# Attention probabilities turned by VectorE blocks and transfers instead of TensorE transposes, with the heads spread over the next group

## The reference

```python
def masked_softmax(s, mask):
    s = jnp.where(mask, s.astype(jnp.float32), NEG_INF)
    m = jnp.max(s, axis=-1, keepdims=True)
    p = jnp.exp(s - m) * mask
    return p / jnp.maximum(jnp.sum(p, axis=-1, keepdims=True), TINY)

p_c = masked_softmax(s_c, cmp_end[None, :] <= t[:, None])
o_c = jnp.einsum('bgrsc,bgcd->bgrsd', p_c.astype(vc.dtype), vc)
...
o = g[..., 0:1] * to_heads(o_c) + g[..., 1:2] * to_heads(o_s) + g[..., 2:3] * to_heads(o_w)
```

## Time and profile before

| | |
|---|---|
| median of 3 executions | 2071.82 us (2071.75 to 2071.89) |
| profiled execution | 2071.25 us |
| its span, first to last instruction | 2069.6 us |
| mean granted TensorE clock | 0.998 |
| busy: PE / PEld | 2050.0 / 1703.5 us |
| busy: DVE / ACT / POOL | 1352.3 / 972.7 / 168.6 us |
| read from memory | 379.91 MB, 185 GB/s over the span |

### The profile page before, as it was taken

How to read it: one execution, slowest core, us unless ns; L and a number is a source line. 1 busy time by engine, 2 the same in 40 slices (tenths; PEclk the granted TensorE clock), 3 DMA queues, 4 the chain that set the end, 5 groups by cost and what they waited for, 6 DMA issues and landing times.

```text
span 2069.6 us, 27656 instructions
## 1 busy us (share of the span) xinstructions
PE 2050.0 (99%) x9586; PEld 1703.5 (82%) x9586; DVE 1352.3 (65%) x1783; ACT 972.7 (47%) x1261; POOL 168.6 (8%) x263
## 2 busy tenths in 40 slices
PE   8999999999999999999999999999999999999997
PEld 7788888888888888888888888888888888888886
DVE  6755667666664578886678876766546646655664
ACT  5443545454543455554455544544434434444443
POOL 3000000000000011111011110110000000100000
PEclk9999999999999999999999999999999999999999
DMA  8656464545466656666656567676666666666663
GB/s 268 215 160 199 133 182 141 165 141 167 143 205 198 176 175 186 181 182 201 186 171 183 183 211 255 217 217 215 215 195 213 213 194 194 223 202 180 227 213 134
DMA packets 197145, 396.19 MB, mean 191 GB/s; under 512 B 13408, under 2 KB 13504, under 8 KB 195632
## 3 DMA queue, kind: packets, MB, share of 16 engines
q1 hardware_dynamic: 188656, 364.42, 57.1%
q0 software_dynamic: 8208, 29.75, 4.7%
q10 hardware_dynamic: 176, 0.53, 0.1%
HBM read 379.91 MB, written 2.16 MB: 185 GB/s over the span
## 4 chain that ended last, share of the span: by engine, by line
PE 94%; DVE 2%; issue 2%; ACT 1%; DVEq 0%; DMA 0%; POOLq 0%; POOL 0%; ACTq 0%
PE acc L294 29%; PE acc L296 29%; PE acc L295 29%; PE x L918 1%; PE tr L329 1%; DVE lo L261 1%; PE x L854 1%; PE tr L876 1%; DMA raw<-w_proj_ssm 0%; PE x L861 0%; PE tr L878 0%; PE tr L869 0%; PE tr L881 0%; PE x L930 0%; PE x L329 0%
## 5 line engine op out<-in xcount | busy, mean ns | idle before, releaser
L261 DVE TENSOR_TENSOR lo<-raw,hi 128x1024 fp32r<-128x1024 f32 x688 | 839.3, 1233 | 490.0 <-ACT hi L255 481.1
L255 ACT ACTIVATE hi<-raw 128x1024 fp32r<-128x1024 f32 x688 | 718.6, 1058 | 655.4 <-PE acc L296 610.3
L294 PE MATMUL acc<-hi,LAh 128*128 128x512 f32 x1848 | 734.8, 398 | 1.2 <-DVE lo L261 1.2
L296 PE MATMUL acc<-hi,LAl 128*128 128x512 f32 x1848 | 721.4, 390 | 0.0
L295 PE MATMUL acc<-lo,LAh 128*128 128x512 f32 x1848 | 720.6, 390 | 0.0
L294 PEld LDWEIGHTS acc<-hi,LAh 128*128 128x128 f32 x1848 | 347.3, 188 | 74.0 <-issue 3.6
L296 PEld LDWEIGHTS acc<-hi,LAl 128*128 128x128 f32 x1848 | 347.0, 188 | 72.9
L295 PEld LDWEIGHTS acc<-lo,LAh 128*128 128x128 f32 x1848 | 347.4, 188 | 71.7 <-issue 1.7
L294 PE MATMUL acc<-hi,LBh 128*128 128x512 f32 x896 | 350.1, 391 | 0.7 <-DVE lo L261 0.7
L296 PE MATMUL acc<-hi,LBl 128*128 128x512 f32 x896 | 349.0, 389 | 0.0
L295 PE MATMUL acc<-lo,LBh 128*128 128x512 f32 x896 | 348.9, 389 | 0.0
(11 more groups left out here) (304 smaller groups left out, 1210.6 us busy)
## 6 DMA issues: line engine op xcount, KB each, us to landing
raw<-w_in SPq DMA_DIRECT2D x304, 512.0 KB, 3.8
raw<-w_up SPq DMA_DIRECT2D x128, 512.0 KB, 4.0
raw<-w_down SPq DMA_DIRECT2D x128, 512.0 KB, 4.7
raw<-w_proj_ssm SPq DMA_DIRECT2D x64, 512.0 KB, 4.6
raw<-w_proj_nsa SPq DMA_DIRECT2D x32, 512.0 KB, 4.4
raw<-w_out SPq DMA_DIRECT2D x32, 512.0 KB, 5.1
W<-acs_rows POOLq DMA_DIRECT2D x8, 1024.0 KB, 5.0
W<-TB POOLq DMA_DIRECT2D x48, 128.0 KB, 4.2
```

What stands on the lines that cost most here:

```text
L255: act.activation(hi[:, sl, :, :], raw[:, sl, :, :], ACT.Copy).then_inc(s_hi, 1)
L261: dve.tensor_tensor(lo[:, sl, :, :], raw[:, sl, :, :], hi[:, sl, :, :].bitcast(F32), ALU.subtract).then_inc(s_lo, 1)
L294: pe.matmul(o, xh, wh, start=(k == 0), stop=False)
L296: x = pe.matmul(o, xl, wh, start=False, stop=(k == KT - 1))
```

## The change

PE's transposes of the probabilities go. `PB` now holds, for each half of the tokens, four blocks of 128 keys (the compressed ones, `PC`, are the last block). DVE's `scale_probs` becomes `factors` (only the small operations), ACT scales (`scale_probs`, four instructions), and DVE turns the 32x32 blocks (`turn_probs`, two instructions). POOL issues four transfers of 128 KB for each head (`spread_probs`) that put the blocks on their partitions in `PTS`, which `values` reads through an access pattern of runs of 32 numbers. There is one `PTS` for three groups (in BCT) and one for the last (Y), and the block transposes go to BCT, then TH, then V3.

The steps of a head are spread: after the scores in slot s come the maxima and exponentials in s + 1, the factors in s + 3, the scaling in s + 4, the block transposes in s + 5 and the values in s + 9. Steps beyond slot 31 fall into the next group (`late`). The scores stand in slots 12, 19, 25 and 30, in the last group in 12, 17, 22 and 27. The convolution's turn moves from slot 18 to 17. ACT, DVE and POOL have the stage written out instead of looping.

```diff
-SL_S, SL_PT, SL_PV = (12, 16, 20, 25), (16, 20, 25, 29), (17, 22, 27, 31)
-SL_Q, SL_BC = 10, 18
+SL_S = ((12, 19, 25, 30),) * 3 + ((12, 17, 22, 27),)
+A_MAX, A_SUM, A_MUL, A_TURN, A_PV = 1, 3, 4, 5, 9
+SL_Q, SL_BC = 10, 17
...
+        PC = PB[:, :].rearrange("p (b m k) -> p b m k", b=2, m=4)[:, :, 3, :]
+        PBT = [BCT[:, 8:12, :].rearrange("p k s -> p (k s)")] * 9 + [TH.rearrange("p a s -> p (a s)")] * 3 + [V3[:, 0:2, :].rearrange("p n c -> p (n c)")] * 4
+        PTS = [BCT[:, 12:16, :].rearrange("p k s -> p (k s)")] * 3 + [flat_y]
...
+            def spread_probs(n):
+
+                pool.wait_ge(s_pb, n + 1)
+                if n:
+                    pool.wait_ge(s_tr, 2 * (E_AT + EPV + 6 * ((n - 1) // 4) + (n - 1) % 4) + 2)
+                for a in range(4):
+                    pool.dma_start(PTS[n // 4][:, S * a:S * (a + 1)],
+                                   PBT[n][32 * a:32 * (a + 1), :].rearrange("i (b n) -> i b n", b=4)).then_inc(s_ps, 16)
...
-            def turn_probs(i, r, e):
-                pe_event(pe, e, [(s_p, 4 * i + r + 1)])
+            def values(i, r, e):
+
+                pe_event(pe, e)
+                pe.wait_ge(s_stage, 5 * i + 5)
+                pe.wait_ge(s_ps, 64 * (4 * i + r + 1))
+                pt = PTS[i].rearrange("p (a b m j) -> p b m a j", a=4, b=2, m=4)
                 for b in range(2):
-                    pe.transpose(TR[b][:, 0:P], PB[:, 512 + P * b:512 + P * (b + 1)], identf[:, :])
-                    for k in range(2):
-                        pe.transpose(TR[b][:, P * (k + 1):P * (k + 2)], PB[:, S * b + P * k:S * b + P * (k + 1)], identf[:, :])
-                    pe.transpose(TR[b][:, 384:512], PC[:, b, :], identf[:, :]).then_inc(s_tr, 1)
...
-                    pe.matmul(TR[0][:, 0:S], VSs[:, 0, b, :], PTS[:, b, 0:S], start=(b == 0), stop=False,
+                    pe.matmul(TR[0][:, 0:S], VSs[:, 0, b, :], pt[:, b, 0:2, :, :], start=(b == 0), stop=False,
...
+            def scale_probs(n):
+                act.wait_ge(s_rs, n + 1)
+                for k in range(4):
+                    x = act.activation(probs(k), probs(k), ACT.Copy, scale=SUM[:, k:k + 1])
+                x.then_inc(s_p, 1)
...
+            def turn_probs(n):
+
+                dve.wait_ge(s_p, n + 1)
+                if n:
+                    dve.wait_ge(s_ps, 64 * n)
+                if n == 12:
+                    dve.wait_ge(s_stage, 20)
+                for h in range(2):
+                    x = dve.transpose(PBT[n].rearrange("p (b h m j) -> p h m b j", b=4, h=2, m=4)[:, h, :, :, :],
+                                      PB[:, 512 * h:512 * (h + 1)].rearrange("p (m i b) -> p m b i", m=4, b=4))
+                x.then_inc(s_pb, 1)
```

## The result

The changed kernel takes 2081.4 us (median of 5, 2079.2 to 2082.5) against 2071.75 us (2071.45 to 2071.89, 5): ratio 1.0044, 95% interval 1.0033 to 1.0055. It is slower by more than 0.2%. The forecast of 2072.7 us is 8.7 us too low; the time lies inside the range. The profiled execution took 2081.44 us with a span of 2079.8 us, 10.2 us more than before.

What follows compares the result with a forecast made beforehand. The prediction took TensorE's (PE's) queue as setting the end of the span. Its terms, -14.0 + 0.3 + 14.6 = +0.9 us, added to the median of 2071.82 us, gave 2072.7 us, range 2060 to 2084 us.

Steps and rivals of the forecast that it cites:

- The transposes: Attention stage on PE: removing eight transposes of every head was to gain 14.0 us, all on the path.
- The strided reading: Value products on PE reading runs of 32 numbers: 0 to 3 us, taken as 0.3 us.
- The totals of DVE: Attention stage: added DVE work, at most +1.1 us a head, was to be hidden in free time, as was ACT's.
- The waits stand in heads 1 and 3: PE before the values in the attention stage: waits only in these heads of each group, 14.6 us in sum.
- the walk: Engine queues followed in order: waits of 1.5 and 1.3 us in three groups, 3.8 and 2.4 in the last.
- The chain of 7.4 us: From the end of DVE's block transposes to the last transfer's landing: 7.1 to 9.1 us, taken as 7.4.
- rival 1: Attention stage: the chain is in time, about 3 us of waits stay, 2061 us, at best 2058; chance 0.29.
- rival 2: Transfers collide with weight loads and land in 8.45 us, eight waits 1 us longer: 2081 us; slower cases together 0.28.
- head 3 of the last group: PE before this head's values: 5.0 us of room for the transfers, so a wait of 2.4 us.
- rival 3: PE's clock falls in waits: 2077 us after the last group's two, 2092 after all eight; slower cases together 0.28.
- nothing outside the stage changes: Rest of the kernel outside the attention stage: no change in time, priced at nothing.
- The likeliest case: Whole kernel: gains and waits cancel to within 4 us, no change within about 0.2%; chance 0.43.

Runs made afterwards that it cites:

- put right: Kernel with only heads 1 and 3 later, plus head 1's scores in slot 16 and values in slot 26 in the last group: 2063.8 us.
- 16 more: Kernel before with POOL's loop written out and 16 POOL transfers that nothing needs, one of 128 KB a head: 2072.1 us.
- 64 drains ahead: Changed kernel with 64 empty drains added far ahead of the stage in POOL's stream: 2079.65 us.
- transfers from ACT: Changed kernel with each head's four transfers issued by ScalarE, in the slot after the block transposes, instead of POOL: 2075.7 us.
- drains in idle: Changed kernel with one more POOL drain for each head, behind the landing of its four transfers: 2074.2 us.
- values two slots later: Changed kernel with the values 11 slots behind the scores instead of 9 (10 in the last group): 2072.9 us.
- two heads later: Changed kernel with only the values of heads 1 and 3 one slot later (two for head 1 of the last group): 2067.8 us.
- PE kept busy: Changed kernel with 34 transposes of a unit matrix into a free bank before the values of head 15: 2080.5 us.

## Why the prediction was right and wrong

**Right, by its own steps.** The transposes give 14.0 us: 3.46 us a group where nothing else waits. The strided reading costs nothing; 0.3 us was charged. The 390 ns that the Trainium skill gives for a bf16 transpose on TensorE, in "VectorE: DVE Perf Modes", section "The three transpose paths", are not what one costs in a pipelined row: leaving 96 out gave 0.109 us apiece. The totals of DVE (+6.7 us) and ACT (+12.9) are hidden. The waits stand in heads 1 and 3 and nowhere else. In the first three groups they are 8.6 us in sum where the walk gave 8.4, and in head 1 of the last group 3.3 where it gave 3.8. The chain of 7.4 us from the transposes' end to PE was 7.1 to 7.6 us in seven of the eight heads that waited, so rival 1 (in time) and rival 2 (8.45 us everywhere) both fall as sizes. What rival 2 names, transfers that meet the weight loads, is in the 7.1 to 7.6 us all the same (see the last section). An order with one slot more, in which those six waits vanish and nothing else moves, shows that the waits are the transfers' and not PE's own.

**Wrong in size: head 3 of the last group.** 2.4 us were charged and 7.1 came. Its transfers took 8.9 us from the transposes' end where the term was 7.4, beyond the 8.45 us that rival 2 saw as the slow case, and PE came 0.3 us earlier than in the walk (4.7 us behind them, not 5.0): a wait of 4.17 us. It brought rival 3, the lower clock, at 1.6 us in the values and 1.1 us in the next group. The landing scatters: the slowest of its four transfers took 5.7, 5.7, 6.2 and 6.8 us in four kernels with the same work there, the last number in the changed kernel; in the orders of the last group with head 1 later and with it put right it was 7.0 and 6.0 us. Rival 3 came in one of the eight places that it named, and the forecast left it out of the sum; it also came in the scan, behind a wait that nobody had named.

**Wrong: "nothing outside the stage changes".** This step put the price of an edit at nothing and named no cover for it. POOL's 64 issues were costed where they stand, at 0.54 us each, and not at the next drain of the queue, which comes some 165 us later in front of a value that PE needs. It cost 4.4 us, half of the miss. The trace of before had the price, in rows that I did not read. The same drain takes 0.58 us in the six passes from 816 us on, where POOL has issued one transfer since its last drain, and 1.73 us at 763 us, where it has issued 15:

```profile
L594 POOLq DRAIN  x6: 580/584/597, 816.4 to 1164.5; - x6
```

That is 0.08 us for each transfer, and 64 more would have made it some 5 us; 4.6 us came. The 1.41 us of idle time there against 0.28 us in the next pass says the same.

**The sum.** +0.9 was predicted for the span. Add 4.4 us (scan), 4.7 us (head 3 of the last group), -0.6 us (the other waits and strided products) and 0.8 us at two places that differ from run to run, where I know no cause: 10.2 us. The likeliest case, no change within 0.2%, was not what happened, since both misses lie on the same side. That the time lies inside the range is in part luck: the range was built from the walks, the transfers and the strided products, and nothing in it stood for the scan.

**What stays open.** Why the landing for head 15 scatters by 1.1 us. And what POOL does in such a drain: the runs show the price, not the work. The fifteen drains that were added came behind the landing of their transfers; one ahead of it wasn't tried. Nor was it tried to hold a weight load back until POOL has issued all four.

## What to carry to other kernels

Work taken off the engine that sets the end is worth its full length only where every chain behind it has room: count for each head the time from its last step to the consumer, give a slot more to those that lack it and to those alone, and look for bunches on the other engines (2072.9, 2067.8 and 2063.8 us came from nothing but slots). Short transfers that somebody waits for should be issued with no large load between them, from a queue that has time: here SP's, which issues the loads and so keeps them back. If they stay with POOL, put a drain behind them where POOL is idle.

## What the runs showed of the hardware

- **A drain on POOL pays for the transfers POOL has issued since the last one**, 0.07 to 0.08 us each, 5.99 us of standstill for 64, some 160 us after the last one landed. By the number of transfers between two drains of before, after, the runs with 16 more and with 64 drains ahead: 0.58 us for 1, 1.73 for 15, 3.04 for 31, 5.91 for 66 and 6.32 for 79. The last step is smaller than the others (0.03 us each), so the price is not strictly in proportion. The kernels' own end may hold the same bill: POOL's last drain comes behind 99 transfers without a drain between and takes 9.2 us in every run, in before from 2060.2 to 2069.4 us, where SP is done at 2067.6 us.

```profile
L99 POOLq DRAIN  x1: 9209/9209/9209, 2060.2 to 2060.2; - x1
```

  No run tried to shorten that one. The Trainium skill, "DMA: Bandwidth & Descriptors", section "Terms", says that for transfers from GpSimd software writes the descriptors to rings, where SyncE's and ScalarE's go through hardware; that the price is absent with both of these (1.41 us) fits it, and no run shows more than that.
- **Where the transfers stand among the weight loads changes the landing more than the queue does.** The same four transfers of 128 KB land in 3.9 us (median) from POOL, 3.4 from ACT and 2.7 from SP, with 6.8, 5.4 and 4.1 us at most, though the issues are no shorter (567, 627 and 604 ns). But the queue was never changed alone: from SP, which issues the loads too, no load of 512 KB can come between the four. The traces of the seven kernels in which POOL issues them split the same way. Where SP had issued a load since the first of the four, a transfer took 4.2 us or more (4.8 median, 166 transfers), elsewhere 2.8 (median, 282 transfers). Head 0 of the first group has no load among its four, and they land in 2.6 to 2.9 us from POOL; head 1 has loads at 250.74 and 251.85 us, and its four take 2.5, 3.8, 4.4 and 5.4 us. The same page's section "Issuing engine by pattern" says that the hardware path is generally faster; with no load among the four POOL's 2.8 us and SP's 2.7 us differ little, and no run tests the path by itself.
- **The length of an idle time does not decide by itself whether the clock falls.** PE kept its rate behind 2.90 us (after), 2.80 us (transfers from ACT), 2.04 us (drains in idle) and even 3.55 us (values two slots later, in the scan at 769.95 us, with a granted clock of 1.00 from 766 to 776 us). It came out at full rate and fell some 0.7 to 1.2 us later behind 1.93 us (64 drains ahead), 2.22 us (from ACT), 2.86 us (drains in idle) and 3.51 us (two heads later). It was slow from the first products on behind 2.96 us (PE kept busy, head 13), 3.05 us (64 drains ahead), 3.41 us (values later), 3.56 us (after, in the scan) and 4.17 us (after). The timeline behind the 2.86 us:

```profile
571.71 0.67 PE L895 MATMUL tr<-Y,VSs 128*128 128x256 f32 x2 [2.86 <-DMA Y<-V]
572.21 0.38 PE L897 MATMUL tr<-Y,VSs 128*128 128x128 f32 x2
572.43 0.70 PE L895 MATMUL tr<-Y,VSs 128*128 128x256 f32 x2
572.92 0.64 PE L897 MATMUL tr<-Y,VSs 128*128 128x128 f32 x2
```

  The two products of 128 columns take 0.38 us and then 0.64. Such a stretch costs some 1.6 to 3 us on top of the wait.
